# Retention layer of a hybrid decode step: 32 steps written out, and the sample of each step worked one step later

## The reference

```
def step(s, inp):                         # of one chunk, for every head
    decay  = exp(where(mask, diff, -inf))
    scores = einsum('bihd,bjhd->bhij', qc, kc) * decay
    intra  = einsum('bhij,bjhe->bihe', scores, vc)
    cross  = einsum('bihd,bhde->bihe', qc, s) * exp(cum)[..., None]
    s_new  = exp(cum[:, -1, :])[..., None, None] * s + einsum('bjhd,bjh,bjhe->bhde', kc, tail, vc)
    return s_new, intra + cross
...
o = (_rms(o).reshape(b, L, RET_VW) * head_norm).astype(h.dtype)
return (o * silu(gate)) @ w_out, s_new
```

## Time and profile before

| | |
|---|---|
| median of three runs | 2263.56 us |
| the profiled execution's own time | 2265.41 us |
| its span in the trace | 2263.6 us |
| TensorE busy, of the span | 2099.0 us (93%) |
| VectorE, ScalarE, GpSimd busy | 1265.8, 856.6, 384.0 us |
| the retention steps (first transpose to the next phase's first instruction) | 576.9 to 888.2 us |

### The profile page before, as it was taken

One profiled execution on the slowest core, in us unless ns is written; L12 is line 12 of the kernel. 1 busy time (PEld: TensorE's weight loads), 2 busy tenths in 40 slices (PEclk: granted clock), 3 DMA queues, 4 the chain that ended last, 5 costly groups with the idle time before them and its releaser, 6 DMA issues. The chain is left out here.

```text
span 2263.6 us, 42045 instructions
## 1 busy us (share of the span) xinstructions
PE 2099.0 (93%) x14150; PEld 1905.8 (84%) x14150; DVE 1265.8 (56%) x1894; ACT 856.6 (38%) x1905; POOL 384.0 (17%) x566
## 2 busy tenths in 40 slices
PE   6799999999799997999689999999999999967998
PEld 6799999999567665888489999998999999855886
DVE  7999655665233356323144757675767667663331
ACT  7221221332222234223254545454545545463331
POOL 0200000000121221000001424343443333320000
PEclk9899999999899998999899999999999999978999
DMA  4323433332778788243432333332332333355340
GB/s 127 115 80 113 116 97 109 102 97 69 236 229 261 235 278 296 74 137 108 108 82 61 87 89 80 80 95 72 91 91 78 84 97 78 86 184 155 109 126 28
DMA packets 388682, 274.01 MB, mean 121 GB/s; under 512 B 119761, under 2 KB 344241, under 8 KB 388457
## 3 DMA queue, kind: packets, MB, share of 16 engines
q1 hardware_dynamic: 340342, 242.77, 36.8%
q10 hardware_dynamic: 48144, 28.76, 4.1%
HBM read 184.59 MB, written 86.88 MB: 120 GB/s over the span
## 5 line engine op out<-in xcount | busy, mean ns | idle before, releaser
L1512 PE MATMUL p3acc_ps<-xn2hi,p3whi 128*128 128x272 f32 x1536 | 463.3, 302 | 21.6 <-DVE xn2lo L2226 14.8
L1512 PE MATMUL p3acc_ps<-xn2lo,p3whi 128*128 128x272 f32 x1536 | 447.4, 291 | 0.0
L1512 PE MATMUL p3acc_ps<-xn2hi,p3wlo 128*128 128x272 f32 x1536 | 447.3, 291 | 0.0
L257 PE MATMUL p1ps<-x1hi,w1hi 128*128 128x272 f32 x1288 | 374.2, 291 | 13.5 <-DVE y1out L592 10.3
L257 PE MATMUL p1ps<-x1hi,w1lo 128*128 128x272 f32 x1288 | 373.7, 290 | 0.0
L257 PE MATMUL p1ps<-x1lo,w1hi 128*128 128x272 f32 x1288 | 372.8, 289 | 0.0
L1512 PEld LDWEIGHTS p3acc_ps<-xn2hi,p3whi 128*128 128x128 f32 x1536 | 294.1, 191 | 23.3 <-DVE xn2lo L2226 14.9
L1512 PEld LDWEIGHTS p3acc_ps<-xn2lo,p3whi 128*128 128x128 f32 x1536 | 294.3, 192 | 0.2
L1512 PEld LDWEIGHTS p3acc_ps<-xn2hi,p3wlo 128*128 128x128 f32 x1536 | 293.7, 191 | 0.0
L257 PEld LDWEIGHTS p1ps<-x1hi,w1hi 128*128 128x128 f32 x1288 | 244.4, 190 | 14.1 <-issue 14.1
L257 PEld LDWEIGHTS p1ps<-x1hi,w1lo 128*128 128x128 f32 x1288 | 244.7, 190 | 0.0
(11 more groups left out here) (297 smaller groups left out, 4157.7 us busy)
## 6 DMA issues: line engine op xcount, KB each, us to landing
w1raw<-in_ret_w_in SPq DMA_DIRECT2D x48, 512.0 KB, 4.9
p3raw<-in_ssm_w_in SPq DMA_DIRECT2D x48, 512.0 KB, 4.3
ret_vg<-y1out SPq DMA_DIRECT2D x32, 512.0 KB, 3.2
r_vg<-ret_vg SPq DMA_DIRECT2D x32, 512.0 KB, 4.6
r_sin<-in_state_ret SPq DMA_DIRECT2D x32, 512.0 KB, 5.9
out_ret_sample<-r_sout ACTq DMA_DIRECT2D x32, 512.0 KB, 6.0
s_cr<-sums SPq DMA_DIRECT2D x64, 256.0 KB, 3.4
ret_qk<-y1out SPq DMA_DIRECT2D x16, 512.0 KB, 3.7
```

Of the source, the lines that this page charges most:

```text
L257: last = nc.tensor.matmul(bank[:, 2 * at + i, 0:HB], w[s][:, idx, k, :], x[:, idx, k, i * HB:(i + 1) * HB], start=(k == 0 and j == 0), sto ...
L1512: last = nc.tensor.matmul(pr_ps[:, n % 2, 0:TB], wt[:, j % 2, k, :], x[:, k, b * TB:(b + 1) * TB], start=(k == 0 and i == 0), stop=(k == K ...
```

## The change

All of it is in `phase_retention` and the constants that it reads.

1. The old state of a sample is split too: ScalarE copies `r_sin` to a high part (`state_high`), VectorE subtracts it to get the low part (`state_low`), both 128x1024, in place in a region of w2hi that is free until the end of the phase. The cross product then multiplies the queries, also split, by each part: four fp32r products of 512 columns in place of two float32 ones. The queries' tile `qm` holds the high parts in columns 0 to 63 and the low parts in 64 to 127 of a 128-wide block.
2. The sample of step t-1 is worked in step t, between `states` and `squares`/`chunk_rows`; before, the sample of step t stood in step t, behind the scores (the one of c = 0 at the start of step 1).
3. The samples' own scores product is added into `r_cr` (once in a head), `crs` has 128 rows, and the sample rows are four products by `pairs`, which adds the two halves; they are made in step 1 of the next head.
4. `r_sout` has two buffers, and the samples' gated rows have one of their own.
5. All 32 steps are written out: no loop, no registers.

```
-        nc.tensor.matmul(cr_ps[0:cols.shape[1], :], cols, s_in[:, s, k, :], ...)      # sample(h, c), after the scores
+                def sample(x):
+                    h, c = divmod(x, NCH)
+                    pe.wait_ge(s_low, x + 1)
+                    if c == 0:
+                        pe.wait_ge(q_own, h + 1)
+                        wait(pe, cr_ev, h)
+                    for k in range(NK):
+                        for part in (s_hi, s_lo):
+                            last = nc.tensor.matmul(cr_ps[:, :], qm[:, k, c * P:(c + 1) * P], part[:, k, :], ...)
+                    if c == 0:
+                        last = nc.tensor.matmul(cr_ps[0:NS, :], scs[:, :], vs, start=False, stop=False)
+                    last.then_inc(cr_mm, 1)
+                    pe.wait_ge(k_own, x + 1)
+                    wait(pe, sb_add, x)
...
+                def sample_rows(h):
+                    for p in range(NV):
+                        last = nc.tensor.matmul(y_ps[:, p, 0:NS], crs[:, p * P:(p + 1) * P], pairs[:, :], start=True, stop=True)
...
+                for t in range(STEPS):                                                   # TensorE
+                    if c == 1 and h:
+                        sample_rows(h - 1)
+                    if following:
+                        turn_chunk(t + 1, sums)
+                    states(t)
+                    if t:
+                        sample(t - 1)
+                    ...
+                        squares(chunk_y(t - 1), P, turned, turned - 1 if following else turned)
+                    chunk_rows(t)
+                    if following:
+                        chunk_scores(t + 1, sums)
+                    if c == 0:
+                        if h:
+                            squares(chunk_y(t), P, turned, turned)
+                        turn_samples(h, sums)
+                        scores(samples_turn(h), sums, qs, kks[:, :, 0, :], NS)
...
+                def state_high(x):                                                       # ScalarE
+                    dma_wait(act, state_in[x % 2], x // 2 + 1)
+                    wait(act, cr_mm, x)
+                    nc.scalar.activation(s_hi, s_in[:, x % 2, :, :], ACT.Copy).then_inc(s_high, 1)
...
+                    if c != 1 and t:
+                        own(t - 1)
+                    if following:
+                        prepare(t + 1)
+                    if t:
+                        state_high(t - 1)
+                        take_sums(t - 1)
+                    if t >= 2:
+                        store_sample(t - 2)
+                    square(chunk_y(t), P)
...
+                def state_low(x):                                                        # VectorE
+                    dve.wait_ge(s_high, x + 1)
+                    nc.vector.tensor_tensor(s_lo, s_in[:, x % 2, :, :], s_hi, ALU.subtract).then_inc(s_low, 1)
...
+                    if t >= 2:
+                        sample_state(t - 2)
+                    if t:
+                        state_low(t - 1)
+                    if c:
+                        next_state(t)
+                    gate(t)
+                    if t + 1 < STEPS:
+                        chunk_decay(t + 1)
```

More of the change, by code:

```diff
@@ new lines, in chunk_scores, with squares @@
+                def chunk_scores(t, sums):
+                    scores(chunk_turn(t), sums, qk[:, t % SL, 0:NK, :], qk[:, t % SL, NK:2 * NK, :], P)
+                def squares(m, r, turned, scored):
+                    pe.wait_ge(k_ev, turned)
+                    pe.wait_ge(sc_ev, scored)
+                    pe.wait_ge(sq_sum, m + 1)
+                    wait(pe, ss_ev, m)
+                    nc.tensor.matmul(ss_ps[:, 0:r], ones[:, :], sq[:, 0, 0:r], start=True, stop=True).then_inc(ss_mm, 1)
@@ new lines, in states, with chunk_rows @@
+                def states(t):
+                    n = chunk_turn(t)
+                    pe.wait_ge(k_ev, n + 1)
+                    pe.wait_ge(v_ev, n + 1)
+                    wait(pe, st_add, t)
+                    for k in range(NK):
+                        last = nc.tensor.matmul(st_ps[:, k, :], kt[:, t % 2, k * P:(k + 1) * P], v[:, t % 2, :],
+                                                start=True, stop=True)
+                    last.then_inc(st_mm, 1)
+                def chunk_rows(t):
+                    h, c = divmod(t, NCH)
+                    pe.wait_ge(sc_ev, chunk_turn(t) + 1)
+                    wait(pe, gated, chunk_y(t))
+                    if c:
+                        pe.wait_ge(q_dec, 7 * h + c)
@@ L997, in group @@
-                    squares(n - 1, P, turned, turned)
-                turn_chunk(0, 0, -1)
-                scores(prep(0, 0), 0, qk[:, 0, 0:NK, :], qk[:, 0, NK:2 * NK, :], P)
+                        last = nc.tensor.matmul(y_ps[:, p, :], v[:, t % 2, cols], sc[:, t % 2, :], start=True, stop=(c == 0))
+                        if c:
+                            for k in range(NK):
+                                last = nc.tensor.matmul(y_ps[:, p, :], S[:, k, cols], qd[:, t % 2, k, :],
+                                                        start=False, stop=(k == NK - 1))
@@ L1145, in _ @@
                 pool.wait_ge(zeroed, 2)
-                prepare(0, 0)
-                group(0, first=True)
-                with pool.Fori(1, RH - 1) as h:
-                    group(h)
-                group(RH - 1, more=False)
+                for t in range(STEPS):
+                    h, c = divmod(t, NCH)
+                    if c == 1 and h:
+                        add_squares(samples_y(h - 1), NS)
+                    if t + 1 < STEPS:
+                        prepare(t + 1)
+                    add_squares(chunk_y(t), P)
+                    if c == 0:
+                        queries_low(h)
```

663 lines of the change are left out of this document (324 added, 339 removed).

## The result

| | before | after |
|---|---|---|
| Time, median (lowest to highest) | 2262.85 us (2261.09 to 2264.79, 4 runs) | 2342.99 us (2341.61 to 2347.36, 4 runs) |
| Profiled execution: its time, its span | 2265.41, 2263.6 us | 2343.4, 2341.6 us |
| TensorE busy, share of the span | 93% | 89% |

The ratio is 1.0357, with a 95% interval of 1.0339 to 1.0375: 80 us slower, where 96 were forecast. The time lies in the range and in the case that was taken as the likeliest.

A forecast was written before the change was run, and what follows sets the result against it. TensorE was taken as the bound, busy 58.41 of 59 us in head 0's steps. Terms 48 + 25 + 9 + 2 + 7 + 5 = 96 us on 2265.41 gave 2361, less 2 for the median: 2359 us, range 2310 to 2420.

The forecast's parts named there:

- the case that was taken as the likeliest: Whole kernel: both waits of TensorE uncovered, forecast 2359 us, by itself 2330 to 2395 us; chance 72%.
- TensorE's work per step: Steps inside a head: four cross-product records fall from 0.43 to 0.24 us, saving 0.77 us, to 7.62 us of work.
- The two waits uncovered: Each step: TensorE waits 1.75 us before the turn of keys and 1.69 before the sample; step 11.04 us, was 8.39.
- High and low part by the nearest rows: State split in each step: ScalarE's high part takes 1.03 us and VectorE's low part 1.22, from similar 128x1024 operations.
- Inside the heads: Heads 0 to 2, between rows of c = 1 and c = 7: 18 steps at +2.65 us, 48 us more.
- The last head: Weights' low parts precede the state's on VectorE: step 12.5 us against 8.39, 25 us more over six steps.
- The clock: In the steps: idle stretches lower TensorE's clock in every sixth to tenth step, +3 to +8 us, taken as 5.
- Boundaries, start, end: Three head boundaries cost 9 us, the start 2 for sample 0's split, the end 7 for sample 31.
- The stores: Second `r_sout` buffer removes VectorE's 22.2 us of waiting for stores, off TensorE's path: worth nothing.
- shorter steps: Rival: both waits stay covered, TensorE stays the bound at 7.62 us a step, 2248 us in total; chance 6%.
- The clock did not stay down: Rival it denies: gaps hold TensorE at 1.2 GHz for good, 2480 us, or in every second step, 2420; chance 10%.
- One wait instead of two: Rival: one wait of about 1.7 us goes, steps 9.3 us, total 2300 to 2320 us; chance 9%.

## Why the prediction was right

All in all: the path, both waits and their order were right, and the sizes were off in both directions. Measured less forecast is -10 us inside the heads, +6.5 in the last head, -2 to -3 each at the boundaries, the start and the end, and -5 for the clock, whose cost is in the last head's time already. The sum came within 16 us, in part by luck, since the last head's error offsets others.

*TensorE's work per step*: right. 7.62 us were forecast, and 7.58 is a step in which nothing waits.

*The two waits uncovered*: the mechanism is right, both by the rows after and by the experiments that took one or both away. The size was too high: 1.75 and 1.69 us against 1.39 to 1.60 (PE's and the weight loads' readings) and about 1.2 (states' end at 694.68 to 695.89). The term that failed is the hand-off, the time from one engine's end to the start of the engine that waits for it. From VectorE's scores to TensorE I used 0.29 us, and measured are 0.10 (692.62 to 692.72); from the turn of keys to ScalarE 0.22, measured 0.03 (693.13 to 693.16); from the low part to TensorE 0.29, measured 0.05 (695.84 to 695.89). The 0.62 us of these three, less 0.09 that the sample took more than I had summed, make 0.53 of the 0.56 us between 11.04 and 10.48. Over 18 steps that is 10 us. The step lies below the bounds of 11.0 and 11.4 that I gave, since they varied the two durations and left the hand-offs fixed. The value came from the only place of the kernel before where TensorE waited for the scores. In that kernel each such wait is followed by an instruction that counts it up on another semaphore (`held`), and three of them stand before the turn of keys; in the changed kernel the waits are bare. Written out but with `held` kept, the old kernel still has the long hand-off at that place:

```profile
663.40 0.28 DVE L1158 TENSOR_TENSOR r_sc<-r_misc,r_dec 128x128 f32<-128x128 f32 x1
...
664.01 0.41 PE L902 MATMUL r_misc<-r_ident,r_kks 128*128 128x128 f32 x2 [1.07 <-DVE r_sc L1158]
```

That is 663.68 to 664.01, 0.33 us. So the loop isn't the cause. The next wait of the same boundary says the same: from ScalarE's copy of the samples' keys to TensorE's samples' scores it is 0.29 us in that kernel (665.80 to 666.09), with `held`, and 0.06 in the changed one (676.73 to 676.79), with bare waits. That `held` is the cause is what remains, but no kernel was run that drops it alone: argued, not shown. ScalarE's 0.22, read at the same place, would have the same cause.

*High and low part by the nearest rows*: right. 1.03 and 1.22 us were taken from copies and sums of the same size in another phase; measured are 1.05 and 1.22.

*Inside the heads*: 48 us forecast, 38.2 measured, by the hand-offs.

*The last head*: 12.5 us a step and 25 in all forecast, 31.5 measured, 13.64 a step. That is 5.25 more than before in each, above the bounds of 3.6 and 4.7. The chain itself came out right: the cross product starts 7.49 us after the scores (897.67 to 905.16), forecast 7.7. What I left out here is the clock: the sample behind the wait takes 1.31 us longer (3.28 against 1.97) in each of the six steps, 8 us.

*The clock*: 5 us were forecast, spread over all steps; inside the steps it cost about 8, all of it in the last head. In heads 0 to 2 it stays at 1.00 through steps with idle stretches of 1.39 and 1.05 us; I had charged a fall in every sixth to tenth. In the last head, with the idle stretch at 2.9 to 3.5 us, it fell in every step, and with both splits moved (1.39 and 1.05 us again) it fell in none. I had set the Trainium skill's rule aside ("TensorE: Matmul & The Clock Gate", section "Why this matters for your kernels": no loss as long as no long unbroken idle gap stands between bursts), because of one stretch at a boundary. The changed kernel's own steps agree with it: 1.00 with the gaps short, 0.50 after the long one. Other stretches do not: with the weights' low parts later the clock fell in two of six steps though no idle stretch in them was over 1.81 us, and it fell at some boundaries behind 1.44 us. There the measurement decides. The length of the idle stretch alone does not tell whether the clock falls, and what else does is open. My own reading of the earlier trace rows was also off: I called the busy time before the fall mostly products of 64 columns, but of its 3.41 us 1.94 went to products of 512 (652 to 653.94), and 1.47 to those of 64.

*Boundaries, start, end*: 9, 2 and 7 us forecast, 6.7, -0.4 and 4.4 measured. At the boundaries the new place's cost is net of a gain that I did not see: in the old place the same code is 3.6 to 6.8 us shorter than before at each, of which 1.2 is sample 0's product moved into a step. Differences as small as 3 us, and the start's, lie within what one execution differs from another there.

*The stores*: worth nothing, as said, and shown by the run with two buffers.

*The rivals*: shorter steps is what the same kernel does with the sample in its old place, so its price per step was real (7.58 us against 7.62) and its condition false; its total, 2248 us, was 14 too high, by what the boundaries gain. The clock did not stay down: in heads 0 to 2 no step has it at 0.50. One wait instead of two came out at 2327 where its high part was put first, above the 2300 to 2320 given, since the last head kept its full length and one step of each other head waited for a load; its plain steps, 9.57 us, are near the 9.3 given.

## What to carry to other kernels

A product on the bound engine can be cover for other engines' chains: before it is moved, follow each chain that ran beside it from its release to its next use, and price the move by what then shows. An edit that saves time on the bound engine by lengthening such a chain (here a split into two parts) has either sign, by its place. Take a hand-off's latency from a wait of the same form as the changed kernel will have. And read differences between two traces only in stages that repeat from one execution to the next.

## What was not expected of the hardware

- In the changed kernel a wait that really binds costs little: 0.10 us from VectorE's end to TensorE's start, 0.05 from the low part to the cross product, 0.03 from TensorE's modelled end to ScalarE.
- TensorE kept its full clock with two idle stretches of 1.39 and 1.05 us in each 10.48 us, and dropped to 1.2 GHz for the products behind an idle stretch of 2.92 us. Behind equal idle stretches of 1.81 us it did either, in one and the same kernel (the weights' low parts later).
- The fastest of these kernels, the changed one with the sample behind the scores, has little left on two sides: head 0's steps keep TensorE busy for 44.41 of 45 us, and in the last head the DMA share is 0.97.

```profile
601.00:646.00 45.00, 44.41 (x282) 36.17 (x281) 25.40 (x28) 18.06 (x35) 9.15 (x14) 1.00 0.88 272
798.00:845.00 47.00, 44.94 (x276) 35.57 (x274) 40.62 (x41) 29.54 (x45) 9.82 (x16) 1.00 0.97 340
```
